# One core, two transformer blocks in fp32: the split of a weight chunk set behind the evictions at two boundaries, and one sum of weights made by an adding transfer

## What is computed

```
def hybrid_layer(x, ..., w_out, norm_ffn, w_ff1, w_ff2):
    ...
    x = x + mixed @ w_out
    u = jax.nn.relu(rmsnorm(x, norm_ffn) @ w_ff1)
    return x + (u * u) @ w_ff2
```

## Time and profile before

| | |
|---|---|
| median of 3 runs | 2901.3 us (2901.23 to 2902.55) |
| the profiled execution | 2901.05 us |
| its span | 2899.2 us |
| granted TensorE clock, mean | 0.999 of full speed |
| PE busy | 2865.8 us (99%), 16106 matmuls |
| DVE busy | 1694.2 us (58%) |
| ACT busy | 1227.6 us (42%) |
| POOL busy | 74.0 us (3%) |
| moved by DMA | 320.93 MB, mean 111 GB/s |

### The profile page before, as it was taken

One profiled execution on the slowest core, in us unless ns is written; L12 is line 12 of the kernel. 1 busy time (PEld: TensorE's weight loads), 2 busy tenths in 40 slices (PEclk: granted clock), 3 DMA queues, 4 the chain that ended last, 5 costly groups with the idle time before them and its releaser, 6 DMA issues.

```text
span 2899.2 us, 38609 instructions
## 1 busy us (share of the span) xinstructions
PE 2865.8 (99%) x16106; PEld 2365.9 (82%) x16106; DVE 1694.2 (58%) x2470; ACT 1227.6 (42%) x1882; POOL 74.0 (3%) x63
## 2 busy tenths in 40 slices
PE   7999999999999999999999999999999999999999
PEld 6878887888887777888888877888888877888887
DVE  6776666655255656533335764666674663656677
ACT  5555422235233333532224455454444455444444
POOL 0000011110000000000000000000000000000000
PEclk9999999999999999999999999999999999999999
DMA  8443355542432222232332222224423222234323
GB/s 303 169 136 117 117 189 181 189 135 92 98 102 67 78 69 74 71 104 96 100 102 84 85 87 73 88 102 131 131 81 101 77 84 73 88 117 131 103 88 115
DMA packets 224637, 320.93 MB, mean 111 GB/s; under 512 B 16496, under 2 KB 123344, under 8 KB 223568
## 3 DMA queue, kind: packets, MB, share of 16 engines
q1 hardware_dynamic: 207504, 266.96, 28.7%
q0 software_dynamic: 11888, 49.29, 5.4%
q10 hardware_dynamic: 5072, 2.23, 0.3%
HBM read 308.98 MB, written 2.11 MB: 107 GB/s over the span
## 4 chain that ended last, share of the span: by engine, by line
PE 94%; DVE 2%; ACT 2%; DMA 1%; issue 1%; SPq 0%; DVEq 0%; ACTq 0%
PE G L2396 49%; PE G L2403 17%; PE G L2349 5%; PE G L2455 5%; PE G L2438 4%; PE X L2349 4%; PE X L2722 1%; DMA raw<-in_hgrn_w_in 1%; PE G L2421 1%; PE X L2500 1%; PE X L2736 1%; PE X L2822 1%; PE X L2832 1%; PE G L2778 1%; PE X L2733 1%
## 5 line engine op out<-in xcount | busy, mean ns | idle before, releaser
L2396 PE MATMUL G<-u_hi,w_hi 128*128 128x512 f32 x2096 | 835.7, 399 | 6.9 <-issue 6.9
L2396 PE MATMUL G<-u_hi,w_lo 128*128 128x512 f32 x2096 | 818.1, 390 | 0.0
L2396 PE MATMUL G<-u_lo,w_hi 128*128 128x512 f32 x2096 | 817.5, 390 | 0.0
L1438 DVE TENSOR_TENSOR w_lo<-raw,w_hi 128x2048 fp32r<-128x2048 f32 (+3 forms) x210 | 471.8, 2248 | 456.5 <-ACT w_hi L747 455.6
L747 ACT CAST w_hi<-raw 128x2048 fp32r<-128x2048 f32 (+3 forms) x214 | 401.8, 1878 | 450.9 <-DMA raw<-in_w_ff 171.7
L2396 PEld LDWEIGHTS G<-u_hi,w_hi 128*128 128x128 f32 x2096 | 393.9, 188 | 94.4 <-issue 14.6
L2396 PEld LDWEIGHTS G<-u_hi,w_lo 128*128 128x128 f32 x2096 | 393.9, 188 | 84.7
L2396 PEld LDWEIGHTS G<-u_lo,w_hi 128*128 128x128 f32 x2096 | 394.4, 188 | 78.8 <-issue 1.4
L2236 DVE TENSOR_TENSOR hid_f<-silu_g,G 128x512 f32<-128x512 f32 x44 | 30.1, 687 | 169.9 <-PE G L2396 156.7
L1557 DVE SCALAR_TENSOR_TENSOR acc<-ada_raw,cond,acc 128x512 f32<-128x512 f32 x140 | 105.2, 752 | 13.6 <-DMA ada_raw<-in_ada_w 5.1
L2438 PE MATMUL G<-u_hi,w_hi 128*128 128x256 f32 x384 | 109.2, 284 | 2.8 <-DVE u_lo L1703 2.8
(11 more groups left out here) (512 smaller groups left out, 4722.9 us busy)
## 6 DMA issues: line engine op xcount, KB each, us to landing
raw<-in_ffn_w_in SPq DMA_DIRECT2D x88, 512.0 KB, 4.8
ada_raw<-in_ada_w POOLq DMA_DIRECT2D x40, 1024.0 KB, 5.7
raw<-in_w_ff SPq DMA_DIRECT2D x72, 512.0 KB, 4.4
raw<-in_w_in SPq DMA_DIRECT2D x56, 512.0 KB, 4.1
raw<-in_attn_w_in SPq DMA_DIRECT2D x96, 256.0 KB, 3.7
raw<-in_ffn_w_out SPq DMA_DIRECT2D x40, 512.0 KB, 4.7
raw<-in_hgrn_w_in SPq DMA_DIRECT2D x32, 512.0 KB, 5.3
yT<-in_w_ff SPq DMA_DIRECT2D x28, 512.0 KB, 7.5
```

The costliest lines, as they stand in the source:

```text
L1438: tt(w_lo[slot][:, 0:nk, 0:w], raw[slot][:, 0:nk, 0:w], w_hi[slot][:, 0:nk, 0:w].bitcast(F32), ALU.subtract).then_inc(s_lo, 1)
L2396: ins = mm(G[0:c1_ - c0, m, :], w[iw][:, k, c0:c1_], xs[ix][:, x0(b) + kk, :], start=first, stop=last, skip_group_check=True)
```

## The change

Three things, all within the seven parts described above.

1. At the first block of `ff_in00` and `ff_in10` (`in_two`), the second chunk's split comes later: on ACT behind the four squares and ahead of the `upper` steps, on DVE behind the sums of tiles 0 and 1 and ahead of the first `lower`.
2. W12 += W22 is no longer made by DVE (line 1445) but by a second adding transfer, which POOL issues ahead of the one it had. ACT's cast of W12+W22 and DVE's W11 += W12 wait for that transfer. Counts of the semaphores are changed to suit.
3. In `hidden_sums` the calls of `lower` are written in another place in the loop.

```
-                    pool.wait_ge(s_wsum, 3 * q + 2)
+                    for j in range(2):
+                        pool.wait_ge(s_quad[j], 64 * (q + 1))
+                    pool.dma_start(W12, W22, accum_op=ALU.add).then_inc(s_fourth, 16)
+                    pool.wait_ge(s_wsum, 2 * q + 1)
                     pool.wait_ge(s_lo, c0 + B21 + 1)
                     pool.dma_start(W21, W11, accum_op=ALU.add).then_inc(s_fourth, 16)
...
-                elif i == B_SUM4:
-                    act.wait_ge(s_fourth, fourth0 + 16 * (q + 1))
+                elif i in (B12_22, B_SUM4):
+                    act.wait_ge(s_fourth, fourth0 + 32 * q + (16 if i == B12_22 else 32))
...
                 for b in range(2):
-                    for s in range(g["chunks"]):
-                        split(name, b, s)
                     in_two = b == 0 and name in HEADS
+                    split(name, b, 0)
+                    if not in_two:
+                        split(name, b, 1)
...
                     if in_two:
+                        split(name, b, 1)
                         for m in range(3):
                             act.wait_ge(s_ff, squared + m + 1)
                             upper(b, m)
...
                 if i == B12_22:
-                    for j in range(2):
-                        dve.wait_ge(s_quad[j], 64 * (q + 1))
-                    tt(W12, W12, W22, ALU.add).then_inc(s_wsum, 1)
-                    dve.wait_ge(s_wsum, 3 * q + 1)
+                    dve.wait_ge(s_fourth, fourth0 + 32 * q + 16)
                     dve.wait_ge(s_lo, c)
                     tt(W11, W11, W12, ALU.add).then_inc(s_wsum, 1)
...
                 for b in range(2):
-                    for s in range(g["chunks"]):
-                        split(name, b, s)
+                    in_two = b == 0 and name in HEADS
+                    split(name, b, 0)
+                    if not in_two:
+                        split(name, b, 1)
                     for m in range(4):
                         t = 4 * b + m
+                        if in_two and m == 2:
+                            split(name, b, 1)
+                        if m > 1:
+                            lower(b, m - 2)
...
-                        if m:
-                            lower(b, m - 1)
+                    lower(b, 2)
                     lower(b, 3)
```

More of the change, by code:

```diff
@@ L308, in build @@
         s_in = sem("small_inputs_landed")
-        s_ada = [sem("ada_landed0_then_fourth_sums"), sem("ada_landed1")]
+        s_ada = [sem("ada_landed0_then_weight_sums"), sem("ada_landed1")]
         s_ada_first = [[sem(f"first_ada_landed{p}_{i}") for i in range(2)] for p in range(ADA_FIRST)]
@@ L753, in weights_upper @@
                     act.wait_ge(s_quad[1 if i == B21 else 0], 64 * (q + 1))
-                elif i == B_SUM4:
-                    act.wait_ge(s_fourth, fourth0 + 16 * (q + 1))
+                elif i in (B12_22, B_SUM4):
+                    act.wait_ge(s_fourth, fourth0 + 32 * q + (16 if i == B12_22 else 32))
                 else:
-                    act.wait_ge(s_wsum, 3 * q + 1 + (B12_22, B_SUM3, B11_12).index(i))
+                    act.wait_ge(s_wsum, 2 * q + 1 + (B_SUM3, B11_12).index(i))
                 sc.copy(w_hi[c % SLOTS][:, :, :], weights_of[i]).then_inc(s_hi, 1)
@@ L1452, in weights_lower @@
                     dve.wait_ge(s_lo, c + 1)
-                    dve.wait_ge(s_wsum, 3 * q + 2)
+                    dve.wait_ge(s_wsum, 2 * q + 1)
                     tt(W12, W11, W22, ALU.subtract).then_inc(s_wsum, 1)
```

## The result

The changed kernel took 2916.3 us (median of 4 runs, 2911.4 to 2919.2) against 2901.9 us (4 runs, 2901.2 to 2903.7) beside it: 1.0046 times as long, interval 1.0033 to 1.0058. It is slower, by 13 to 14 us, and outside my range, which ended at 2912.5. The profiled execution took 2919.2 us, at the upper end of these runs. Later sections compare it with the profiled 2901.05 us of before.

A forecast was written before the change was run, and what follows sets the result against it. PE was taken as the bound, busy 2865.8 of 2899.2 us. Third-product delays of 6.7 us plus 0.7 for restarts took the profiled 2901.05 to 2908.45 us, on the median 2908.7 us; range 2902.0 to 2912.5.

The forecast's parts named there:

- my 5.3: PE's idle time at the two boundaries before b = 1, 2.4 + 2.9 us, which the later split would remove.
- The delayed chunk: Second chunk at the first boundary: lower part done near 1930.4, PE needs it at 1934.0, delay covered by 3.6 us.
- The row model: DVE from W11 += W12: first sum 4.4 us behind, 15.0 us more to the third product's lower part, PE 0.2 later.
- The terms before the third product: Delays of the third product's start in seven parts, 6.7 us in all, plus 0.7 us for PE's restarts.
- 0.7 us later: First part: third product starts at 1959.0 against 1958.32, although PE comes 2.4 us earlier.
- 0.3 us later: Fourth part, behind the second boundary: delay of the third product's start by the same rows.
- about 3 us: PE's expected wait for DVE's `w_lo` before the third product in the first and fourth part.
- the 0.1 us of the restart: Cost of each restart of PE, 0.31 us to the next matmul in place of 0.227; 0.7 us for seven.
- the time from landing to landing: From the last quarter's landing to the new transfer's, taken as 7.5 us; each microsecond moves the sum by 7.
- Rival 4: New transfer takes a microsecond longer than the old, following right behind 2 MB of loads: 2915.7 us, chance 0.09.
- the four chances within 0.2%: Chances 0.07 + 0.09 + 0.08 + 0.02, given as 0.25, for a time within 0.2% of no change.
- rival 1: Transfer lands within 5.5 us in place of 7.5, so a 2.28 us DVE instruction is truly saved: 2897.8 us, chance 0.09.

The follow-up runs named there:

- the split alone: Against the changed kernel, W12 += W22 goes back to DVE and the split stays behind the evictions: 2904.8 us, ratio 1.0003 to the kernel before.
- the transfer alone: Against the changed kernel, both splits go back ahead of the evictions and the new adding transfer stays: 2911.8 us, ratio 1.0025 to the kernel before.
- the kernel with PE kept busy: Changed kernel plus 18 and 12 overwritten matmuls on PE ahead of the third product in parts 1 and 4: 2913.6 us, ratio 1.0033 to the kernel before.
- the repetition: The changed kernel run again without any edit: 2914.8 us, ratio 1.0048 to the kernel before.
- the early issue: Against the changed kernel, W12 and W21 land on separate semaphores, so the new transfer no longer waits for W21: 2898.4 us, ratio 0.9983 to the kernel before.

## Why the prediction was wrong

**Right: direction, place and mechanism.** Both boundary gaps went (2.53 and 2.96 us of shift for my 5.3). The delayed chunk was in time, no wait stands within b = 1. They came back before the third product because DVE's row hangs on the transfer; the split alone shows that half, the transfer alone the other. The row model held to 0.1 us: 4.4 and 15.0 us in the first part and the second, and issue to landing 6.9 to 7.0 us in the five parts without a boundary. The terms before the third product, restart included, were:

| us | 1st | 2nd | 3rd | 4th | 5th | 6th | 7th | sum |
|---|---|---|---|---|---|---|---|---|
| predicted | 0.8 | 1.5 | 1.3 | 0.4 | 0.8 | 1.4 | 1.2 | 7.4 |
| measured | 2.4 | 1.3 | 1.0 | 0.5 | 0.9 | 1.4 | 1.5 | 9.0 |

**Wrong, first: no term for the clock.** The sum priced PE's wait before the third product in the first and the fourth part as the difference of two idle times, "0.7 us later" and "0.3 us later". But the idle time of 2.4 us at the boundary, which had not brought the clock down in that execution, was joined to the delay of the same part, into 4.85 and 3.37 us in one piece, and there it fell: 2.2 and 2.9 us, 5.1 in all. This is the largest miss, and the evidence for it was in my own text, which forecast "about 3 us" of waiting in both places; the execution that I read had no fall behind its idle times of 2.4 and 2.9 us, and I took the 0.1 us of the restart for longer ones too. By my own terms the two idle times would have been 3.1 and 3.2 us, where a fall is likely and not certain: behind the two of 3.2 us of the split alone there was one. The first part's was longer because of the third point below. Without falls, by the ratio of the kernel with PE kept busy (1.0033 of 2901.9), the time would have been near 2911.5 us, inside my range but 2.8 us above the forecast (interval 2908 to 2915).

**Wrong, second: "Behind the third product the remaining chunks had slack of a microsecond or more and shift with it."** In the third and the seventh part DVE has three additions more (3.5 us) ahead of the last lower part. DVE and PE at the last product of the seventh part, before and after:

```profile
2887.32 2.29 DVE L1450 TENSOR_TENSOR w_lo<-tmp,w_hi 128x2048 fp32r<-128x2048 f32 x1
2889.53 1.28 DVE L1470 TENSOR_TENSOR h_by_token<-h_by_token,X 128x512 f32<-128x512 f32 x2
...
2890.31 0.47 PE L2349 MATMUL X<-w_hi,hidden_sums_hi 128*128 128x512 f32 x1
```
```profile
2905.46 2.29 DVE L1452 TENSOR_TENSOR w_lo<-tmp,w_hi 128x2048 fp32r<-128x2048 f32 x1
2907.67 1.28 DVE L1472 TENSOR_TENSOR h_by_token<-h_by_token,X 128x512 f32<-128x512 f32 x2
...
2908.45 0.47 PE L2356 MATMUL X<-w_hi,hidden_sums_hi 128*128 128x512 f32 x1 [1.33 <-DVE w_lo L1452]
```

In both, PE starts 0.70 us behind the end of the lower part: before, too, this product was bound by DVE. What it waits for last is not that lower part, which the profile names, but the instruction behind it: the first of the two additions that take the fifth product out of PSUM (0.7 us each). The seventh product writes into the same bank X, and PE waits for that addition (`s_add`). What hid this row before was that PE began the third product 1.0 us behind its weights (2868.41 against 2867.41). Now it begins at once, PE's four products from there take 21.8 us, DVE's row 22.9 us (23.4 in the seventh part of the changed kernel, whose old adding transfer took 7.35 us in place of 6.91), and the difference comes out as later starts of 0.72 and 1.38 us, 2.1 in all. The same happens with the transfer alone (0.8, 1.4).

**Wrong, third: one price for seven transfers.** "The unknown is the time from landing to landing" was right as a warning, but I took 7.5 us from the earlier trace rows for each, 6.9 of it from issue to landing and 0.6 ahead of the issue. In the first part issue to landing took 8.7 us (9.3 from landing to landing), and 8.8 in the repetition, so that PE came 1.7 us later there; in the fourth part it took 7.5 (8.0 from landing to landing; issue to landing 9.2 in the kernel with the additional matmuls). With the splits ahead of the evictions it took 7.1 and 6.9 us in these two parts, with the early issue 7.3 and 7.4. The long ones have in common that they are issued while DVE is at its row of short additions for the lower parts, which goes on for 1.6 to 2.0 us behind the issue (1.0 us with the splits ahead); but the 7.5 us of the fourth part of the changed kernel had 1.8 us of it too, and with the early issue that row went on for 4.7 us behind the issue of a transfer of 7.3 us. So this is a trail and no cause; it stays open. Rival 4 had a longer transfer in all seven parts; it was one. The rule of the Trainium skill, "DMA: Bandwidth & Descriptors", section "Anatomy of one DMA — SWDGE (gpsimd) path", which I had set against the row, gives 4.4 us for this size (estimate); every one of the new transfers took 6.9 to 9.2.

**The balance.** 7.4 forecast, plus 1.6 before the third products (as much as the first part's longer transfer), 5.1 by the clock, 2.1 at the seventh products and 2.0 before the parts give 18.2. On medians the loss is 14.4 us: the 2.0 are no part of the change, and the clock's part is probably smaller in other executions (two of the four ran at a mean clock of 0.998 in place of 0.996; neither was profiled). All misses had the same sign, the clock's alone is in this execution larger than the 3.8 us from my forecast to the range's end, and that range had room for errors of the one row only. A slip without weight: the four chances within 0.2% add up to 0.26 and not to 0.25.

**What I should have seen as a way out:** the prediction counted "all four quarters" as the condition for the transfer, from the diff, and priced rival 1 by a shorter transfer. The wait for W21 is not in the data but in the pairing of two loads on one semaphore. Without it the transfer starts 3.1 us earlier relative to the loads, and the whole change wins 5 us over before.

## What to carry to other kernels

An instruction taken off a half-idle engine and given to a transfer moves nothing by its busy time; compare when its result is there, from the last of its inputs to the first of its readers, and make the issue wait for those inputs alone, on a semaphore of their own. When two idle times of PE may run together, price the longer one with the clock's fall behind it (here 1.6 to 2.9 us each), and look at every later wait that the old slack had covered, not only at the next.

## What was not expected of the hardware

- **The clock after short idle times.** By the traces of all kernels here, idle times of PE of 3.37, 3.47, 4.85, 4.92, 5.25 and 5.29 us were each followed by a fall of the clock (0.50 where the windows above cut it out). Of two of 3.2 us one was (the third product took 7.2 us in place of 5.4), of six of 2.4 to 2.9 us four. Nearly the same idle time at the same place of the program gives either, so a price read from a single execution is one of two values.
- **GpSimd beside DVE.** An addition of 128x2048 fp32 on GpSimd took 4.6 to 5.4 us against DVE's 2.28, and held a DVE instruction with two inputs from 0.42 to 4.64 us.
- **An adding transfer's time** of 1 MiB within the core's memory depends on its surroundings by 2.3 us (6.9 to 9.2): 8.7, 8.8 and 8.7 us at one place in three executions (the changed kernel twice, and the one with additional matmuls), 9.2 once, 6.9 to 7.0 at most other places and 7.1 to 7.9 at the rest, for a reason that stays open.
